# Attention in a two-block transformer kernel: an item's value products ahead of the next item's transposes in TensorE's program

## What is computed

```python
s_loc = einsum('bnqkgd,bnjkd->bnkgqj', qb, kb) * scale      # 128 queries x up to 384 keys
s_loc = where(mask, s_loc, -inf)
s_ctx = einsum('bnqkgd,bjkd->bnkgqj', qb, k_ctx) * scale    # x 256 context keys
p = softmax(concatenate([s_loc, s_ctx, sink_col], -1), -1)
o = einsum('bnkgqj,bnjkd->bnqkgd', p[..., :span], vb) + einsum('bnkgqj,bjkd->bnqkgd', p[..., span:span+L], v_ctx)
```

## Time and profile before

| | |
|---|---|
| median of 3 runs | 2542.04 us (2538.47 to 2542.34) |
| profiled execution, its own time | 2545.86 us |
| its span in the trace | 2544.0 us |
| TensorE (PE) busy over the span | 2473.7 us, 97% |
| VectorE (DVE), ScalarE (ACT), GpSimd (POOL) busy | 1685.1, 1095.7, 1179.5 us |
| attention (steps of all 128 items) | about 321 to 614 us from the span's start |

### The profile page before, as it was taken

How to read it: one execution, slowest core, us unless ns; L and a number is a source line. 1 busy time by engine, 2 the same in 40 slices (tenths; PEclk the granted TensorE clock), 3 DMA queues, 4 the chain that set the end, 5 groups by cost and what they waited for, 6 DMA issues and landing times.

```text
span 2544.0 us, 32112 instructions
## 1 busy us (share of the span) xinstructions
PE 2473.7 (97%) x11857; PEld 1986.7 (78%) x11857; DVE 1685.1 (66%) x1944; ACT 1095.7 (43%) x1746; POOL 1179.5 (46%) x715
## 2 busy tenths in 40 slices
PE   7999999999999999999999999999999999998997
PEld 5778778887778888887886777777878788887885
DVE  5674278897277656649988211224189988889987
ACT  4652467877253332334334221234244444434434
POOL 0225122673475555557565211114476655556564
PEclk8999999999999999999999999999999999999999
DMA  7453010243312222225223111002312222235221
GB/s 300 133 200 82 23 50 18 74 106 136 94 56 83 98 101 83 79 96 206 92 75 117 33 34 42 26 33 89 127 42 75 96 78 83 76 120 217 87 80 66
DMA packets 78071, 235.89 MB, mean 93 GB/s; under 512 B 8764, under 2 KB 12988, under 8 KB 77789
## 3 DMA queue, kind: packets, MB, share of 16 engines
q1 hardware_dynamic: 77916, 233.84, 27.1%
HBM read 180.59 MB, written 39.85 MB: 87 GB/s over the span
## 4 chain that ended last, share of the span: by engine, by line
PE 83%; DVE 9%; issue 3%; ACT 2%; POOL 1%; DMA 1%; SPq 0%; DVEq 0%; ACTq 0%; POOLq 0%
PE S L549 12%; PE S L550 12%; PE S L914 10%; PE S L918 10%; PE S L915 9%; PE S L952 3%; PE S L953 3%; PE S L956 3%; PE MM L786 2%; PE S L786 2%; PE S L760 1%; PE S L761 1%; PE MM L774 1%; DVE xt L1999 1%; PE S L774 1%
## 5 line engine op out<-in xcount | busy, mean ns | idle before, releaser
L2563 POOL TENSOR_TENSOR wbl<-rf,wbh 128x512 fp32r<-128x512 f32 x256 | 397.4, 1559 | 249.2 <-ACT wbh L1416 249.0
L2440 POOL TENSOR_TENSOR wl<-raw,wh 128x1024 fp32r<-128x1024 f32 x58 | 146.9, 2534 | 547.0 <-ACT wh L1160 547.0
L2563 POOL TENSOR_TENSOR wbl<-wq,wbh 128x512 fp32r<-128x512 f32 (+1 forms) x168 | 254.8, 1522 | 174.8 <-ACT wbh L1416 174.5
L1416 ACT ACTIVATE wbh<-rf 128x512 fp32r<-128x512 f32 x256 | 158.5, 628 | 298.9 <-PE S L918 218.4
L914 PE MATMUL S<-th_t,wbh 128*128 128x512 f32 x640 | 251.5, 393 | 0.8 <-issue 0.6
L918 PE MATMUL S<-tl_t,wbh 128*128 128x512 f32 x640 | 250.9, 392 | 0.0
L915 PE MATMUL S<-th_t,wbl 128*128 128x512 f32 x640 | 250.2, 391 | 0.0
L549 PE MATMUL S<-hh,wh 128*128 128x512 f32 x448 | 191.3, 427 | 11.1 <-DVE gt L2371 3.7
L952 PE MATMUL S<-ph,wbh 128*128 128x512 f32 x472 | 187.9, 398 | 7.5 <-DVE xt L2146 4.8
L914 PE MATMUL S<-th_b,wbh 128*128 128x512 f32 x480 | 189.9, 396 | 2.8 <-DVE cu L2043 2.1
L1416 ACT ACTIVATE wbh<-wq 128x512 fp32r<-128x512 f32 (+1 forms) x168 | 99.2, 595 | 214.1 <-PE S L956 119.2
(11 more groups left out here) (392 smaller groups left out, 6058.2 us busy)
## 6 DMA issues: line engine op xcount, KB each, us to landing
mr<-in_w_modT SPq DMA_DIRECT2D x32, 512.0 KB, 4.7
wq<-in_w_d SPq DMA_DIRECT2D x64, 256.0 KB, 5.6
xq<-hid SPq DMA_DIRECT2D x16, 1024.0 KB, 5.1
rf<-in_w_f1g SPq DMA_DIRECT2D x22, 512.0 KB, 3.5
rf<-in_w_f1u SPq DMA_DIRECT2D x22, 512.0 KB, 3.2
hid<-pr SPq DMA_DIRECT2D x22, 512.0 KB, 2.6
rf<-in_w_f2g SPq DMA_DIRECT2D x22, 512.0 KB, 3.3
rf<-in_w_f2u SPq DMA_DIRECT2D x22, 512.0 KB, 3.2
```

The costliest lines, as they stand in the source:

```text
L1416: e.activation(flat(wbh[wslot(f, n)][:, :, :])[:, 0:x.shape[1]], x, ACT.Copy).then_inc(*w_hi.mark((f, n)))
L2440: e.tensor_tensor(l, raw[:, w % 3, 0:n], h.bitcast(F), ALU.subtract).then_inc(*w_lo.mark(w))
L2563: e.tensor_tensor(l, x, h.bitcast(F), ALU.subtract).then_inc(*w_lo.mark((f, n)))
```

## The change

In each step TensorE issues `weigh(i - 3)` and then `turn_weights(i - 2)`, the other way round than before. No instruction is added or removed, and no other engine's program changes.

```diff
@@ -800,10 +800,10 @@
                     join(i - 5)
                 if 1 <= i < 5:
                     keep_warm(i - 2 if i > 1 else 1, 8)
+                if 3 <= i < NI + 3:
+                    weigh(i - 3)
                 if 2 <= i < NI + 2:
                     turn_weights(i - 2)
-                if 3 <= i < NI + 3:
-                    weigh(i - 3)
             SL.back = [[(a_out, NI - 1)], [(a_out, NI - 2)], [(d_ot, NI - 2)]]
             ML.back = [[(d_ot, NI - 1)], [(d_ot, NI - 1)]]
```

## The result

| | before | after |
|---|---|---|
| median of the runs | 2542.19 us | 2652.42 us (2649.9 to 2654.77, 4 runs) |
| ratio | | 1.0429, 95% interval 1.0415 to 1.0442 |
| profiled execution, own time and span | 2545.86, 2544.0 us | 2652.41, 2650.6 us |
| high part of item 2 to that of item 127 | 268.60 us | 378.57 us |

What follows compares the result with a forecast made beforehand. TensorE was taken to bound the attention; after the change, 125 links (3.12 us with five tiles) plus disturbances gave 378.5 us against 268.6, plus 0.7: loss 110.6, median 2652.6 us, range 2638 to 2688 (87%).

Steps and rivals of the forecast that it cites:

- The ring: Five-tile attention step: high part 0.71, 0.03, low part 0.81, 0.15, value products 0.67, transposes to next high part 0.75; 3.12 us.
- W to T: On TensorE, start of value products to start of transposes: taken as 0.67 us, bounds 0.58 and 0.83.
- third rival: In the attention, ready transposes pass waiting value products, so the change does nothing: 2542 us; chance 2%.
- The sum: Attention, high part of item 2 to that of item 127: 378.5 us against 268.6 before; loss 110.6 with 0.7 ahead.
- the two disturbances: In the attention, ScalarE's table load with logarithms adds 1.3 us and VectorE's normalisation adds 1.4.
- Nothing behind the attention: Later stages are runs of matrix products and cannot take the loss back; that stretch stays as long as before.
- The clock: TensorE in the attention, still some 0.8 us in 3.12, keeps the full granted clock, the 2.4 GHz level.
- the row of 8.50 us: End of the attention before the change: 6.47 us busy, 2.03 idle, granted clock 1.00; used to forecast full clock.
- first rival: TensorE's clock swings in the attention: 2712 us with half of the links at the lower level, 2771 with all; 9%.
- opposite rival: The change makes the attention faster, TensorE being bare work, 2.04 in place of 2.17: -6 us, 2536; chance 2%.
- TensorE's own work: Matrix work per five-tile attention step before the change: 2.15 us in kind A, 2.04 of 2.17 in B.
- The comparison of 1.70 with 0.93: Attention step after the change: high part, low part and handovers 1.70 us, against 0.93 of join and scores as cover.

## Why the prediction was right, point by point

- **The ring.** 3.12 us by its terms, 3.11 in the timeline shown. W to T, the one term that no row of before showed, was taken as 0.67 and measured 0.66. That the ring is the cause is shown from four sides: work put into the wait is free and beside it costs in full, one term taken out (0.84 us) brings the turn to 2.26, cover taken away adds what it covered (112 us with the clock kept up, 106 by the terms), and half of the steps cost half. The third rival is out as well: no transposes passed a W that waited, T starts 0.66 us behind it.
- **The sum.** 378.5 us from item 2 to item 127, 378.57 measured. So close a hit is partly luck: the two disturbances were put at 1.3 and 1.4. At the table load the links were 4.15 and 3.95 us (561.20, 565.35, 569.30), 1.0 and 0.8 above 3.12; the second, with the clock down for a moment (T to high part took 1.31 there, 567.99 to 569.30), was not in the sum. The link with the normalisation took 3.60 us (622.99 to 626.59) where the same link of the head before took 2.72 (598.98 to 601.70), 0.9 more and not 1.4. So 2.7 us were forecast and 2.7 came, made up otherwise. Ahead of item 2 the sum had 0.7 for a later high part; from the high part of item 0 to that of item 2 the two traces differ by 0.6 (6.45 and 7.03 us). The lower bound of W to T was misworked: 5 x 0.12 is 0.60, not 0.58; nothing in the forecast hangs on it.
- **Nothing behind the attention** gives back or adds: the rest moved by 4 us, and from the high part of item 127 to the end the twelve traces lie between 1932.2 and 1937.8 us, in no order that goes with the change.
- **The clock.** The forecast held the row of 8.50 us to be good for 380 us, and it was. The first rival's mechanism exists, as the run with the value products first shows (waits of 1.50 to 1.75 us, clock between 0.50 and 1.00); the change brought waits of 0.81 us in A and 0.93 to 1.05 in B with five tiles, shorter ones with four, and there the clock stayed at 1.00. Where between these it begins was not measured. The Trainium skill, "TensorE: Matmul & The Clock Gate", section "A second HAM failure mode: psum-queue depth-cycling", reports such a swing from frequent short idles between groups of products in one kernel. The run with waits of 1.50 to 1.75 us in each link agrees (mean 0.70); the changed kernel, with 0.81 to 1.05, does not (1.00).
- **The opposite rival was mis-sized.** What failed in the prediction's working is "TensorE's own work" of 2.15 us in A, read off distances between starts. The T to W distance of 0.55 held a wait of 0.08; the ring W, ot, low part of 2.17 us held both kinds, not B alone. TensorE's own work is 2.08 with five tiles throughout, and the second rival's price of 6 us should have been 17, which is what the run without the low part gained (12 with the short ot). The forecast did not rest on it, as the longer ring takes over in the changed kernel.
- **The comparison of 1.70 with 0.93** is short by 0.20. `join` can start 0.55 us after the start of T, but ScalarE starts only 0.75 after it, so the cover of 0.93 stood against 1.90. The difference of 0.97 is what a step of five tiles lost (3.12 less 2.15); 0.77 would have given too little. The forecast was right because it summed the ring, with the 0.75 in it, and not this difference.

No version that computes the full result and beats the kernel before came out of this. What is left to gain from the kernel before, 12 to 17 us by these two runs, needs the sum ot shorter or the low part off VectorE's ring, and no order that does this with the full result was tried.

## What to carry to other kernels

In a loop with several items in flight, the place of an instruction in its engine's queue is measured by what stands between it and its producer: add up the hops through the other engines, from the moment at which the queue could go on, here 0.20 + 1.70 = 1.90 us, and compare them with the work that covers them, here 2.15 us before and 0.93 after. What is short, 0.97, is paid in every step, since the next item's producer waits behind. A cover that is long enough does not settle it: before the change, W waited a little all the same, for a low part that stood behind ot in VectorE's queue. A distance between two starts on a busy engine may itself hold a wait, even where the profile lists none. It shows where a start comes exactly one handover (here 0.15) behind the end of its producer; a few idle instructions put beside it tell how much of the distance is work.

## What the runs showed of the hardware

TensorE kept its full clock for 210 us in which it stood still for about 0.8 us in every 3.12 (73% listed busy), and in B with waits of 0.93 to 1.05 (1.00 from 570 to 724 us). Behind one wait of 2.05 us it fell (0.67 over 566 to 570 us). With waits of 1.74 us in every link (1.50 with four tiles) the granted clock swung between its levels and averaged 0.70 over 590 us, and filling 1.30 us of each wait with idle products brought it back to 1.00. There, more products on TensorE made the kernel 114 us faster.
